# Local attention in a hybrid decoder trunk: the weights of its first two tiles turned on VectorE instead of TensorE

## The reference

```python
def swa_mixer(q, k, v, q_g, k_g, sinks, slopes):     # window 128, tiles of 128 tokens
    ...
    s = einsum('bgrnij,bgnjd', q, kb) * d ** -0.5    # a tile against itself and the tile before
    s = where(valid, s - m_h * dist, -inf)           # valid: 0 <= dist < 128
    mx = maximum(max(s, axis=-1), sink)
    p = exp(s - mx)
    p = p / (sum(p, axis=-1) + exp(sink - mx))
    o = einsum('bgrnij,bgnjd->bgrnid', p, vb)
...
yb = swa_mixer(bq, bk, bv, ...) * silu(bz)
y = concatenate([ya, yb, yc, yd], axis=-1)
return x + einsum('btm,md->btd', y, w_out)
```

## Time and profile before

| What | us |
|---|---|
| Median of 3 runs | 1739.8 |
| Lowest and highest | 1739.74, 1739.94 |
| The profiled execution | 1739.26 |
| Its span, first to last instruction | 1737.5 |
| TensorE busy in it | 1733.1 |
| VectorE busy | 1217.9 |
| GpSimd busy | 920.4 |
| ScalarE busy | 489.6 |

### The profile page before, as it was taken

One profiled execution on the slowest core, in us unless ns is written; L12 is line 12 of the kernel. 1 busy time (PEld: TensorE's weight loads), 2 busy tenths in 40 slices (PEclk: granted clock), 3 DMA queues, 4 the chain that ended last, 5 costly groups with the idle time before them and its releaser, 6 DMA issues.

```text
span 1737.5 us, 23503 instructions
## 1 busy us (share of the span) xinstructions
PE 1733.1 (100%) x8904; PEld 1427.6 (82%) x8904; DVE 1217.9 (70%) x2766; ACT 489.6 (28%) x933; POOL 920.4 (53%) x863
## 2 busy tenths in 40 slices
PE   9999999999999999999999999999999999999999
PEld 7788888888888887888887888888888888878887
DVE  7876887847653589886567879778366535898852
ACT  6212323122232434222212132231322233342220
POOL 5555544545555545455565555455455555445454
PEclk9999999999999999999999999999999999999999
DMA  7666655646565766566875665556465567666656
GB/s 272 181 193 200 190 168 161 183 146 189 170 193 179 220 196 206 180 196 194 265 227 180 190 213 182 159 166 185 146 192 171 172 192 219 204 196 184 211 184 208
DMA packets 106881, 332.99 MB, mean 192 GB/s; under 512 B 11632, under 2 KB 23056, under 8 KB 106256
## 3 DMA queue, kind: packets, MB, share of 16 engines
q1 hardware_dynamic: 44224, 155.73, 28.6%
q0 software_dynamic: 40320, 146.82, 28.2%
q10 hardware_dynamic: 22224, 28.94, 5.0%
HBM read 318.85 MB, written 12.60 MB: 191 GB/s over the span
## 4 chain that ended last, share of the span: by engine, by line
PE 98%; DVE 1%; DMA 0%; ACT 0%; issue 0%; SPq 0%
PE acc L659 89%; PE mix L723 3%; PE mix L1016 1%; PE mix L977 1%; PE mix L903 1%; PE mix L929 0%; PE mix L830 0%; PE mix L1080 0%; PE mix L991 0%; DMA w_raw<-in_wstream 0%; PE acc L679 0%; DVE actT_lo L1693 0%; PE mix L840 0%; PE mix L693 0%; PE mix L946 0%; PE mix L871 0%
## 5 line engine op out<-in xcount | busy, mean ns | idle before, releaser
L585 POOL TENSOR_TENSOR w_lo<-w_raw,w_hi 128x512 fp32r<-128x512 f32 x574 | 759.6, 1326 | 565.9 <-DMA w_hi<-in_wstream 435.1
L659 PE MATMUL acc<-w_hi,actT_hi 128*128 128x512 f32 x1408 | 555.6, 395 | 0.0
L659 PE MATMUL acc<-w_hi,actT_lo 128*128 128x512 f32 x1408 | 548.4, 389 | 0.0
L659 PE MATMUL acc<-w_lo,actT_hi 128*128 128x512 f32 x1408 | 548.3, 389 | 0.0
L659 PE MATMUL acc<-actT_hi,w_hi 128*128 128x512 f32 x872 | 342.0, 392 | 0.3 <-DVE actT_lo L1693 0.3
L659 PE MATMUL acc<-actT_lo,w_hi 128*128 128x512 f32 x872 | 339.3, 389 | 0.0
L659 PE MATMUL acc<-actT_hi,w_lo 128*128 128x512 f32 x872 | 339.2, 389 | 0.0
L659 PEld LDWEIGHTS acc<-w_hi,actT_hi 128*128 128x128 f32 x1408 | 264.4, 188 | 56.5 <-issue 2.9
L659 PEld LDWEIGHTS acc<-w_hi,actT_lo 128*128 128x128 f32 x1408 | 264.3, 188 | 55.6
L659 PEld LDWEIGHTS acc<-w_lo,actT_hi 128*128 128x128 f32 x1408 | 264.5, 188 | 52.5
L557 POOL DMA_DIRECT2D w_hi<-in_wstream x280 | 159.6, 570 | 238.8 <-PE acc L659 229.8
(11 more groups left out here) (309 smaller groups left out, 1675.5 us busy)
## 6 DMA issues: line engine op xcount, KB each, us to landing
w_raw<-in_wstream SPq DMA_DIRECT2D x287, 512.0 KB, 4.2
w_hi<-in_wstream POOLq DMA_DIRECT2D x280, 512.0 KB, 3.6
out_x<-slots ACTq DMA_DIRECT2D x7, 1024.0 KB, 7.2
slots<-in_x ACTq DMA_DIRECT2D x4, 1024.0 KB, 6.2
slots<-out_x ACTq DMA_DIRECT2D x4, 1024.0 KB, 7.1
slots<-in_x SPq DMA_DIRECT2D x2, 1024.0 KB, 8.0
slots<-rows ACTq DMA_DIRECT2D x2, 1024.0 KB, 8.1
hops<-slots ACTq DMA_DIRECT2D x2, 1024.0 KB, 5.9
```

Of the source, the lines that this page charges most:

```text
L585: pool.tensor_tensor(w_lo[:, n % RING], w_raw[:, g % RAW, k], w_hi[:, g % HI, k].bitcast(F32), ALU.subtract).then_inc(w_ready, 1)
L659: last = nc.tensor.matmul(bank, lhsT, rhs[:, cs], start=(k == 0 and i == 0), stop=(k == kts - 1 and i == 2))
```

## The change

For tiles 0 and 1 of local attention TensorE's transposes of the weights (`pt0`, `pt1`) are gone, in both layers. In their place VectorE turns the weights from `W["SB"]` in SBUF with 16 block transposes of 32x128.

- Tile 0: the 16 transposes write `W["PT"]` directly; VectorE's copy `PT1` and ScalarE's copy `PT0` are gone, and `pv` waits for VectorE alone.
- Tile 1: the 16 transposes (step `turn`) write the second half of `W["SB"]`; VectorE waits for them, and `PTp` and `PTo` read from there instead of PSUM. The block turns of tile 0's output, 8 of them ahead of `den` before and 8 behind `normalise`, now all 16 stand behind `normalise`, ahead of `y0`.
- Tiles 2 and 3 are as before, but for line numbers.

The diff:

```diff
@@ swa_pe, swa_act, swa_dve: the lists of steps
-        out += ([f"{t-1}.pv"] if t else []) + [f"{t}.{x}" for x in "s0 s1 pt0 pt1".split()]
+        out += ([f"{t-1}.pv"] if t else []) + [f"{t}.{x}" for x in ("s0 s1 pt0 pt1" if t > 1 else "s0 s1").split()]
...
-    return [f"{t}.{x}" for t in T for x in ("gate p0 p1 p2 p3 es" if t else "gate p0 p1 p2 p3 es PT0").split()]
+    return [f"{t}.{x}" for t in T for x in "gate p0 p1 p2 p3 es".split()]
...
-        out += [f"{t}.{x}" for x in ("PT1 y0 y1 y2 y3" if t == 0 else "PTp PTo y0 y1 y2 y3").split()]
+        out += [f"{t}.{x}" for x in ("PT1 y0 y1 y2 y3" if t == 0 else "turn PTp PTo y0 y1 y2 y3" if t == 1 else "PTp PTo y0 y1 y2 y3").split()]
@@ TensorE
-                        pe.wait_ge(B_ACT.sem, B_ACT.at(l, f"{t}.PT0"))
                         pe.wait_ge(B_DVE.sem, B_DVE.at(l, f"{t}.PT1"))
...
-                for i in range(2):
+                for i in range(2) if t > 1 else ():
@@ ScalarE
-                    if t == 0:
-                        w(B_PE, "pt0")
-                        nc.scalar.activation(W["PT"][:, 0:2, 0:P],
-                                             mix[0][:, :].rearrange("p (h c) -> p h c", h=2)[:, :, 0:P], ACT.Copy) \
-                            .then_inc(*s("PT0"))
@@ VectorE
                     turn_blocks("az", [t])
-                    if t:
+                    if t > 1:
                         turn_bz(t - 1, (0, 1))
                     w(B_ACT, "es")
...
-                    w(B_PE, "pt1")
+                    def turn_weights(dst, step):
+                        for r in range(P // BLK):
+                            for f in range(P // BLK):
+                                rs_, fs = slice(BLK * r, BLK * r + BLK), slice(BLK * f, BLK * f + BLK)
+                                last = dve.transpose(dst[fs, :, rs_], W["SB"][rs_, :, fs])
+                        last.then_inc(*s(step))
+
                     if t:
-                        turned = banks[:, 0:2].rearrange("p b (h c) -> p (b h) c", h=2)[:, :, 0:P]
+                        if t == 1:
+                            turned = W["SB"][:, :, P:2 * P]
+                            turn_weights(turned, "turn")
+                            w(B_DVE, "turn")
+                        else:
+                            w(B_PE, "pt1")
+                            turned = banks[:, 0:2].rearrange("p b (h c) -> p (b h) c", h=2)[:, :, 0:P]
                         dve.tensor_tensor(W["PT"][:, :, 0:P], turned, heads(after_all), ALU.mult).then_inc(*s("PTp"))
                         dve.tensor_tensor(W["PT"][:, :, P:2 * P], turned, heads(upto_all), ALU.mult).then_inc(*s("PTo"))
                     else:
-                        dve.tensor_copy(W["PT"][:, 2:4, 0:P],
-                                        mix[1][:, :].rearrange("p (h c) -> p h c", h=2)[:, :, 0:P]).then_inc(*s("PT1"))
+                        turn_weights(W["PT"][:, :, 0:P], "PT1")
                     if t + 1 < TILES:
                         normalise(t + 1)
...
-                        turn_bz(t - 1, (2, 3))
+                        turn_bz(t - 1, (2, 3) if t > 1 else range(P // BLK))
                     w(B_PE, "pv")
```

## The result

| | median, us | lowest, highest | runs |
|---|---|---|---|
| before | 1739.72 | 1738.98, 1740.03 | 22 |
| the change | 1744.28 | 1738.83, 1748.72 | 22 |

The ratio is 1.0027 with a 95% interval of 1.0022 to 1.0033: slower by 4.6 us, where the forecast said 4.9. Two things stand beside that agreement. The change's runs lie 9.9 us apart and those of before 1.1; and TensorE's mean granted clock, 1.000 in the profiled run of before and in all 73 of its runs beside the experiments, reads 0.999 in eleven runs of the change, 0.998 in four and 0.997 in two. The profiled execution took 1743.2 us.

The account below looks back on a forecast made before the run. TensorE, busy 1733.1 of 1737.5 us, was taken to bound the kernel. The sum -1.84 + 3.15 + 3.6 = +4.9 gave 1744.7 us on the median (+0.28%), range 1739.5 to 1747.0.

Parts of the forecast that it names:

- What goes from TensorE: Tiles 0 and 1, two layers: four groups of transposes leave TensorE at 0.46 us each, -1.84 us.
- Tile 0 at price 0: Tile 0: VectorE's 16 added block transposes, 5.04 us, hide in its idle time, cover 1.9 us; no cost.
- Tile 1's list: VectorE's work in tile 1: with nothing in its way, TensorE still waits 0.7 to 0.8 us per layer at tile 2's scores.
- GpSimd's holds: Tile 1: GpSimd's subtractions delay VectorE's SBUF instructions; TensorE waits 3.15 us in the first layer, 3.6 in the second.
- both holds: Tile 1, first layer: `PTo` delayed by one GpSimd subtraction, then `normalise` by the DMA issue and the next subtraction.
- the prediction's own signs: Two TensorE waits of 3 to 4 us at the scores; wrong if 0.8 or absent, or if the 0.23 matmul pitch rises.
- The clock: Rival: TensorE's clock falls after each wait, matmuls at half pace for as long as it waited: +3.4, 1748.1 us; chance 0.08.
- The DMA issue holds too: VectorE's SBUF instruction arriving during GpSimd's DMA issue waits for the next subtraction; rival that it doesn't: 1742.1 us, chance 0.06.
- The row on `den`: Profile row before the change: tile 1's `den` took 1.77 us in place of 0.16, delayed from within GpSimd's DMA issue.

Follow-up runs that it names:

- the version without stands: The change, with four block transposes of the GLA output moved from tile 1's list into VectorE's idle time in tile 0: 1738.09 us, before 1739.75.
- tile 0 alone: Only tile 0's weights turned on VectorE, tile 1 as in the kernel before: 1739.15 us, before 1740.1.
- the last run: The change with tile 1's turned weights through PSUM and 4 of tile 0's 16 block turns behind tile 1's outputs: 1738.03 us, before 1739.68.

## Why the prediction was right, point by point

- **What goes from TensorE, 1.84.** Right: the version without stands is 1.7 under before, and tile 0 alone 0.95.
- **Tile 0 at price 0.** Right. The turn took 5.01 to 5.02 for 5.04, and VectorE idled 2.2 us behind it.
- **Tile 1's list is 0.7 to 0.8 us too long without holds.** The size is right, 0.90 and 0.95 with the turn through PSUM (0.3 of it the longer turn), but "without holds" is wrong: the times of before, on which it rests, hold `nm` for 1.0 us (1.17 for 0.17). In the first layer of the profiled execution, without that hold, the outputs were 0.34 us early.
- **GpSimd's holds: stands of 3.15 and 3.6.** The mechanism is right, and where both holds fall in, the stand is 3.13, 3.13 and 3.12: as forecast in the first layer, 0.5 under the 3.6 of the second. The step that failed is taking this phase for that of every execution. In the profiled one the first layer had no stand: GpSimd's subtraction waits for a DMA and came up 1.7 us later than before ahead of tile 1's turns, and behind `PTo`. By the prediction's own signs this is half a miss: it wanted two waits, and called itself wrong if a wait was absent or the matmul pitch rose behind the stand; one was absent, and the pitch rose to 0.43.
- **The clock.** I gave it 0.08 as a rival to the forecast and priced it at 1.7 per stand. It came on top of the forecast mechanism, not in its place: 17 of 22 runs have a clock under 1.000. From the rounded clocks a mean of 0.0011 is missing, worth some 1.9 us of the mean time (0.0011 x 1741 us = 2.0 us of full clock missing, which at 1.2 GHz is 4.0 us per run; the fall shown above lasted 3.4 us and cost 1.6, so 4.0 / 3.4 x 1.6 = 1.9). The mean of the change's runs is 4.9 over that of before; with 1.84 given back and the clock's 1.9 taken off, the stands took some 4.8 us, where the forecast had 3.15 + 3.6 = 6.75. So the agreement is in part luck: two errors of about 2 us went opposite ways, fewer and shorter stands, and the clock behind them. The page of the Trainium skill that the prediction cited here ("TensorE: Matmul & The Clock Gate", "HAM oscillation — how this bites in real kernels") warned rightly: behind a stand the clock can fall. It fell behind one of two stands each of 3.13, 2.56 and 2.04 us.
- **The spread.** Not forecast. Several instructions of one list, each held or not, and a clock that falls or not, make a time that differs from run to run, here by 9.9 us; with the holds taken away or room made for them the spread was 0.6 to 5.6. The range, 1739.5 to 1747.0, holds the median, but 16 of the 22 runs: one is below it and five are above.
- **The DMA issue holds too.** The rule of the Trainium skill ("SBUF — State Buffer", "Who interferes with whom") would have let the normalisation go; it took 2.03 and 2.15 in these runs, from within the DMA issue to behind the subtraction. The row on `den` was the better guide. The rule's other half, that an instruction with one input in SBUF alone stays clear, the trace agrees with for the copies: with the other input in PSUM they took 0.68 and 0.69 with GpSimd's subtraction beside them. It has an exception that the prediction left out, VectorE's two-port modes. `nm` has one input, in SBUF, and was held (1.17 for 0.17); whether it ran in such a mode no trace here shows.

## What to carry to other kernels

Work that is moved off the engine that bounds costs nothing only as long as its new engine has room ahead of the next wait, and that room has to be counted with the holds in it, not with shares of busy time: VectorE was 70% busy and had no room in that one tile. Times taken from a trace bring that trace's holds with them, so look for a duration that is too long for its shape. When there is no room, look in the same list for work that is ready early and put it into an idle stretch; that turned +4.6 us into -1.7. And when a kernel's runs begin to lie far apart, ask which instructions race for something shared.

## What the runs showed of the hardware

- A stand of TensorE of 3.1 us was followed by a granted clock of 0.72 over 6 us (matmuls at both levels, 0.43 and 0.23 apart), which cost some 1.6 us more; with matmuls on constants in 1.83 us of it, the clock read 1.000 in eleven of eleven runs. With that, 3.7 us more work on the engine that bounds left the median 1.5 us lower.
- Of two stands of the same 3.13 us in one execution, one was followed by a fall of the clock and the other was not; the same holds for two of 2.56 and two of 2.04 us.
- VectorE's block transpose into PSUM took 0.323 us where one into SBUF takes 0.303 (medians of 32), and the copies that read its result from PSUM took 0.66 to 0.69 us in the three traces that have them.
- A hold shifts what stands behind it into the next one: without the hold of the copy (1.1 us), the normalisation's (1.35 us) went as well, in both layers of that trace. In the last run's trace it did not in the first layer (1.78 for 0.68).
- `nm`, with one SBUF input of four numbers a row, took 1.15 to 1.29 us in place of 0.17 in tile 1 of six traces, each time ending with a subtraction of GpSimd that had begun just before it.
